# The up stage of a decoder step: the fourth Winograd product one block later and accumulated in PSUM, weight-quarter sums on VectorE instead of GpSimd

## The reference, cut to what matters

```python
def conv_ffn(hn, buf, w_up, conv_w, conv_b, w_down):
    T = hn.shape[1]
    up = hn @ w_up                                        # (T, 1024) @ (1024, 2 * 2816)
    full = jnp.concatenate([buf.astype(up.dtype), up], axis=1)
    conv = sum(full[:, j:j + T] * conv_w[j] for j in range(CONV_W)) + conv_b   # CONV_W = 3
    a, gt = jnp.split(conv, 2, axis=-1)
    return (a * jax.nn.silu(gt)) @ w_down, full[:, T:]
```

## Time and profile before

| | us |
|---|---|
| median of 3 runs | 2200.4 (2196.86 to 2200.54) |
| profiled execution, its own time | 2205.06 |
| its span, first to last instruction | 2203.1 |
| mean granted TensorE clock | 0.990 of full speed |
| VectorE busy | 1267.4 (58%) |
| ScalarE busy | 754.8 (34%) |
| GpSimd busy | 444.6 (20%) |

### The profile page before, as it was taken

The page is one execution under the profiler, slowest core; times in us unless marked ns, Lnnn a source line. Parts: engine busy times, 40 slices in busy tenths (PEclk is TensorE's granted clock), DMA queues, the critical chain, the costliest instruction groups (busy, mean ns, idle before and its releaser), DMA issues.

```text
span 2203.1 us, 35662 instructions
## 1 busy us (share of the span) xinstructions
PE 2145.4 (97%) x15110; PEld 2090.6 (95%) x15110; DVE 1267.4 (58%) x1576; ACT 754.8 (34%) x1094; POOL 444.6 (20%) x552
## 2 busy tenths in 40 slices
PE   7999999999999999999999999999999999999997
PEld 6999999999999999999999998999999999999997
DVE  6514756335456354236643233489999999864446
ACT  6313334333422322233322034254444444421113
POOL 6689920000000000000000000023232332200001
PEclk9999999999999999999999999999999999999999
DMA  7321215122431223245412143222222222343212
GB/s 274 120 76 65 69 45 186 50 88 78 146 109 67 87 79 108 87 144 180 142 43 77 58 173 154 96 74 72 81 67 81 67 80 82 130 154 125 86 67 77
DMA packets 66419, 222.78 MB, mean 101 GB/s; under 512 B 7584, under 2 KB 13136, under 8 KB 62576
## 3 DMA queue, kind: packets, MB, share of 16 engines
q1 hardware_dynamic: 46432, 130.15, 17.6%
q0 software_dynamic: 14688, 62.06, 7.5%
q10 hardware_dynamic: 5184, 28.98, 3.5%
HBM read 168.38 MB, written 51.78 MB: 100 GB/s over the span
## 4 chain that ended last, share of the span: by engine, by line
PE 71%; DVE 21%; issue 3%; ACT 2%; POOL 2%; DMA 1%; DVEq 0%; POOLq 0%; ACTq 0%
PE ps L305 19%; PE ps L308 19%; PE ps L306 19%; DVE WQ L3170 4%; DVE CA L3218 3%; DVE CA L3217 3%; POOL WX L2711 2%; PE ps L1981 1%; PE ps L2337 1%; PE ps L2313 1%; DVE UBG L2717 1%; DVE HOUT L3227 1%; DVE CA L3220 1%; DVE UBG L3210 1%; DMA WRAW<-in_wslabs 1%
## 5 line engine op out<-in xcount | busy, mean ns | idle before, releaser
L305 PE MATMUL ps<-XH,WH 128*128 128x352 f32 (+1 forms) x1752 | 567.1, 325 | 5.6 <-ACT STAGE L365 3.1
L306 PE MATMUL ps<-XL,WH 128*128 128x352 f32 (+1 forms) x1560 | 492.5, 321 | 0.0
L308 PE MATMUL ps<-XH,WL 128*128 128x352 f32 (+1 forms) x1752 | 371.5, 320 | 0.0
L305 PEld LDWEIGHTS ps<-XH,WH 128*128 128x128 f32 x1752 | 330.5, 189 | 14.3 <-issue 10.2
L299 DVE TENSOR_TENSOR WL<-WRAW,WH 128x1024 fp32r<-128x1024 f32 x133 | 166.7, 1253 | 271.7 <-ACT WH L294 270.2
L306 PEld LDWEIGHTS ps<-XL,WH 128*128 128x128 f32 x1560 | 294.8, 189 | 0.1
L308 PEld LDWEIGHTS ps<-XH,WL 128*128 128x128 f32 x1752 | 292.9, 189 | 0.0
L294 ACT ACTIVATE WH<-WRAW 128x1024 fp32r<-128x1024 f32 x133 | 140.8, 1058 | 330.0 <-PE ps L308 311.9
L305 PE MATMUL ps<-HX,WH 128*128 128x352 f32 (+1 forms) x480 | 153.6, 321 | 4.7 <-DVE HX L3231 3.7
L306 PE MATMUL ps<-HX,WH 128*128 128x352 f32 (+1 forms) x480 | 151.5, 321 | 0.0
L2777 PE MATMUL ps<-B,WQ 128*128 128x258 f32 x528 | 141.0, 288 | 2.9 <-DVE UBG L3210 2.4
(11 more groups left out here) (619 smaller groups left out, 4752.3 us busy)
## 6 DMA issues: line engine op xcount, KB each, us to landing
WRAW<-in_wslabs SPq DMA_DIRECT2D x133, 512.0 KB, 3.6
WRAW<-in_wup SPq DMA_DIRECT2D x88, 256.0 KB, 2.7
scratch_spill<-STAGE SPq DMA_DIRECT2D x40, 516.0 KB, 2.7
ZS<-scratch_spill POOLq DMA_DIRECT2D x24, 516.0 KB, 5.3
scratch_h<-HOUT ACTq DMA_DIRECT2D x22, 516.0 KB, 2.9
HRAW<-scratch_h POOLq DMA_DIRECT2D x22, 516.0 KB, 5.8
XIN<-in_xT SPq DMA_DIRECT2D x8, 516.0 KB, 4.6
XR<-in_xT ACTq DMA_DIRECT2D x2, 2064.0 KB, 8.6
```

The lines of the kernel that those rows point to most:

```text
L305: pe.matmul(out[t], WH[:, slot, w, :], xh(k, t), start=(k == 0), stop=False)
L306: pe.matmul(out[t], WH[:, slot, w, :], xl(k, t), start=False, stop=False)
L308: last = pe.matmul(out[t], WL[:, slot, w, :], xh(k, t), start=False, stop=(k == nk - 1))
```

## The change

- The four weight sums of each quad go from GpSimd to VectorE (`dve_sums`, `dve_late_sums`). A12 - WY is now made before A21 - A11. GpSimd keeps only DMA issues in the stage.
- P1, P6 and P7 of quad f add up in banks 4 and 5 for even f and in 6 and 7 for odd f. P4 of the same quad is added to the same banks, on top of P7. So ScalarE no longer takes P7 and VectorE no longer joins c.
- P4 of quad f runs one quad later, between P5 and P6 of quad f+1, after the join a3 of quad f has read the banks.
- The gate row is scaled in two parts: `scale_gate` its second half in SBUF after a3, `finish_gate` its first half straight out of PSUM after P4, late, between the two convolutions of VectorE's queue. `scale_first` is the value row's scale as before.
- TensorE's order is P1(f), P5(f), P4(f-1), P6(f), P3(f), P7(f), P2(f). It waits for finish_gate(f-2) before P1(f), for d2(f-1) before P5(f), for a3(f-1) before P4(f-1).
- The queues of ScalarE and VectorE are ordered anew, with the counts of the semaphores.

```diff
-            [("P1", 0), ("P5", 0), ("P6", 0), ("P2", 0), ("P3", 0), ("P7", 0), ("P4", 0), ("P1", 1), ("P5", 1),
...
+            [(p, f - (p == "P4")) for f in range(2, NF) for p in ("P1", "P5", "P4", "P6", "P3", "P7", "P2")] +
+            [("P4", NF - 1)])}
...
+        def bank_of(p, f):
+
+            return {"P5": 2, "P3": 2, "P2": 0}.get(p, 4 + 2 * (f % 2))
...
+        def dve_sums(dve, f):
+
+            dve.wait_ge(u_raw[1].sem, u_raw[1].at(16 * (f + 1)))
+            dve.wait_ge(u_raw[2].sem, u_raw[2].at(16 * (f + 1)))
             if f:
+                dve.wait_ge(s_lo, W_AT["P3", f - 1])
+            nc.vector.tensor_tensor(WX, A21, A22, ALU.add).then_inc(s_sum.sem, 1)
+            dve.wait_ge(u_raw[0].sem, u_raw[0].at(16 * (f + 1)))
             if f:
+                dve.wait_ge(s_lo, W_AT["P6", f - 1])
+            dve.wait_ge(s_sum.sem, s_sum.at(4 * f + 1))
+            nc.vector.tensor_tensor(WY, WX, A11, ALU.subtract).then_inc(s_sum.sem, 1)
+
+        def dve_late_sums(dve, f):
+
+            dve.wait_ge(u_raw[3].sem, u_raw[3].at(16 * (f + 1)))
+            dve.wait_ge(s_lo, W_AT["P5", f])
+            dve.wait_ge(s_sum.sem, s_sum.at(4 * f + 2))
+            nc.vector.tensor_tensor(WX, A12, WY, ALU.subtract).then_inc(s_sum.sem, 1)
+            nc.vector.tensor_tensor(A21, A21, A11, ALU.subtract).then_inc(s_sum.sem, 1)
...
+                for f in range(2, 4):
+                    pe.wait_ge(s_lo, i * 14 + W_AT["P1", f])
+                    pe.wait_ge(u_rb.sem, u_rb.at(i * 4 + (2 * f - 2)))
+                    product("P1", f)
+                    pe.wait_ge(s_lo, i * 14 + W_AT["P5", f])
+                    pe.wait_ge(u_dv, i * 6 + DV_AT["d2", f - 1])
+                    product("P5", f)
+                    pe.wait_ge(s_lo, i * 14 + W_AT["P4", f - 1])
+                    pe.wait_ge(u_dv, i * 6 + DV_AT["a3", f - 1])
+                    product("P4", f - 1)
+                    rest_of_quad(i, f)
...
             for f in range(1, NF):
-                act_product_hi(act, "P4", f)
+                more = f < NF - 1
+                if f > 1:
+                    act_product_hi(act, "P7", f)
+                    act_product_hi(act, "P2", f)
+                    act.wait_ge(u_cv.sem, u_cv.at(2 * f - 3))
+                else:
+                    act_take(act, "P1", 1, first_half(UB[1][0]))
+                    act_product_hi(act, "P6", 1)
+                    act_product_hi(act, "P3", 1)
                 now(f - 1, 0)
                 if f > 1:
+                    act_take(act, "P1", f, first_half(UB[f % 2][0]))
+                    if more:
+                        act_product_hi(act, "P1", f + 1)
                     act.wait_ge(u_cv.sem, u_cv.at(2 * f - 2))
...
+                act_take(act, "P5", f, second_half(UB[f % 2][1]))
+                if f == 1:
+                    act_product_hi(act, "P7", 1)
+                    act_product_hi(act, "P2", 1)
+                    act_product_hi(act, "P1", 2)
+                act_product_hi(act, "P4", f)
                 now(f - 1, 1)
...
+                act_take(act, "P6", f, second_half(UB[f % 2][0]))
+                if more:
                     act_product_hi(act, "P5", f + 1)
...
                 silu(f - 1)
...
+                if more:
+                    act_product_hi(act, "P6", f + 1)
                     act_product_hi(act, "P3", f + 1)
...
+            def scale_gate(f):
+                u = UB[f % 2][1][:, 2 + HALF:2 + N]
+                dve.wait_ge(u_dv, DV_AT["a3", f])
+                L(nc.vector.tensor_tensor(u, u, RB[:, HALF:N], M))
+
+            def finish_gate(f):
+                dve.wait_ge(u_pe, U_AT["P4", f])
+                nc.vector.tensor_tensor(first_half(UB[f % 2][1]), pair("P4", f), by_bank(RB[:, 0:HALF]), M).then_inc(u_rb.sem, 1)
...
             for f in range(1, NF):
+                more = f < NF - 1
+                dve_product_lo(dve, "P7", f)
+                dve_product_lo(dve, "P2", f)
+                if more:
+                    dve_product_lo(dve, "P1", f + 1)
+                convolve(f - 1, 0)
+                finish_gate(f - 1)
                 dve_product_lo(dve, "P4", f)
...
                 convolve(f - 1, 1)
...
+                if more:
+                    dve_sums(dve, f + 1)
                 else:
                     slab_lo(0)
...
+                join("d2", f)
+                if more:
+                    dve_product_lo(dve, "P5", f + 1)
+                    dve_late_sums(dve, f + 1)
+                product(f - 1)
+                if more:
+                    dve_product_lo(dve, "P6", f + 1)
+                else:
                     for kk in range(2):
                         rest_h(0, kk)
...
+                join("a3", f)
+                scale_gate(f)
+                if more:
+                    dve_product_lo(dve, "P3", f + 1)
                 else:
                     dve.wait_ge(u_pe, U_AT["P7", f])
                     slab_lo(1)
...
+                join("b", f)
+                scale_first(f)
             for kk in range(2, 4):
                 rest_h(0, kk)
             convolve(NF - 1, 0)
+            finish_gate(NF - 1)
             convolve(NF - 1, 1)
```

More of the change, by code:

```diff
@@ L2729, in pool_ffn @@
                 pool.dma_start(I["spill_x"][:, m, :], XR[:, m, :]).then_inc(xr_out.sem, 16)
[L2730 to L2734, removed]
-            pool.dma_start(O["buf1"], I["buf1"]).then_inc(gl_out, 16)
[L2736 to L2747, removed]
+            pool.dma_start(O["buf1"], I["buf1"]).then_inc(gl_out, 16)
+            pool.wait_ge(h_out.sem, h_out.at(16 * 4))
+            pool.wait_ge(u_pe, U_AT["P6", NF - 1])
+            for kk in range(2):
+                pool_load_h(pool, 0, kk)
+            pool.wait_ge(u_pe, U_AT["P3", NF - 1])
+            for kk in range(2, 4):
+                pool_load_h(pool, 0, kk)
             pool.wait_ge(h_out.sem, h_out.at(16 * 8))
@@ L2773, in product @@
                         k_wait(k)
-                    start, stop = k == 0 and p in ("P1", "P5", "P2", "P4"), k == 3
+                    start, stop = k == 0 and p in ("P1", "P5", "P2"), k == 3
                     for t in range(2):
-                        out, c = ps[:, PAIR[p] + t, 0:HALF // 2], slice(t * (HALF // 2), (t + 1) * (HALF // 2))
+                        out, c = ps[:, bank + t, 0:HALF // 2], slice(t * (HALF // 2), (t + 1) * (HALF // 2))
                         pe.matmul(out, w[:, 0, k, :], x[:, 0, k, c], start=start, stop=False, skip_group_check=True)
@@ L2802, in pe_ffn @@
             evacuated(pe, G_CO + 7)
-            product("P1", slot_of("P1", 0))
+            product("P1", 0)
             pe.wait_ge(s_lo, W_AT["P5", 0])
@@ L2820, in pe_ffn @@
             pe.wait_ge(u_ac, 3)
-            product("P7", slot_of("P7", 0), lambda k: pe.wait_ge(e_lo, E_AT["N3", k]))
+            product("P7", 0, lambda k: pe.wait_ge(e_lo, E_AT["N3", k]))
             norm_samples()
+            pe.wait_ge(s_lo, W_AT["P1", 1])
+            product("P1", 1)
             pe.wait_ge(s_lo, W_AT["P4", 0])
[L2824 to L2843, removed]
@@ L2844, in quad @@
                 if f == 1:
                     pe.wait_ge(norm_rb, 2)
[L2846 to L2853, removed]
-            pe.wait_ge(u_ac, 4 * NF)
+                product("P2", f)
+            rest_of_quad(0, 1)
+            with pe.Fori(0, (NF - 2) // 2) as i:
+                for f in range(2, 4):
[9 more added lines that the diff above has]
+                    rest_of_quad(i, f)
@@ L2856, in pe_ffn @@
+            pe.wait_ge(s_lo, W_AT["P4", NF - 1])
+            pe.wait_ge(u_dv, DV_AT["a3", NF - 1])
+            product("P4", NF - 1)
+            pe.wait_ge(u_rb.sem, u_rb.at(2 * NF - 2))
             pe.wait_ge(u_dv, DV_AT["b", NF - 1])
```

146 lines of the change are left out of this document (56 added, 90 removed).

## The result

| | before | after |
|---|---|---|
| median of 20 runs, us | 2200.26 (2196.86 to 2201.95) | 2203.23 (2199.07 to 2208.29) |
| ratio, 95% interval | | 1.0016 (1.0009 to 1.0023) |
| profiled execution's span, us | 2203.1 | 2199.6 |

The account below looks back on a forecast made before the run. VectorE's queue was taken to set the period, TensorE only following. Terms 1.7 + 2.1 + 1.6 - 0.1 - 1.6 = 3.7 us came off 2200.4, giving 2196.7 us; 8 in 10 range 2184 to 2209.

Parts of the forecast that it names:

- two round trips over ScalarE: Steady quad: VectorE waits for ScalarE's copy of P1(f+2), then for its gate convolution start; idle 1.20 and 0.79 us.
- GpSimd relief: Steady quad: VectorE instructions lengthened beside GpSimd's sums lose 3.0 us a quad, which goes once GpSimd computes nothing.
- three predicted waits: Steady quad: VectorE idle 1.20 us before rest P1 and 0.79 before the second convolution; TensorE's gap 0.7 before P7.
- the ring: Steady quad: the loop of VectorE's queue and its waits over ScalarE that sets the period, forecast at 21.00 us.
- number 3 of the new waits: Steady quad: VectorE's walk from second convolution to next scale_first at 21.00; period 21.09 to 21.00, 1.7 us gained.
- My own sign of being wrong: Steady quads: prediction wrong if the period is off by over 0.2 us, VectorE waits for DMA, or P7 waits drop the clock.
- The start: Start of the up stage: first convolution at 1489.05 instead of 1491.14, 2.1 us sooner, bounds 0 to 4.
- The end: Quad 21's first convolution to the down stage's third group, 32.57 us before: +0.14 us from changed round trips and waits.
- The clock's 1.6 us: Down stage after TensorE's wait for the first residual add: slow clock costs 1.6 us, between 0 and 2.
- The second: Rival: 0.7 us gap before P7 drops TensorE's clock; 2206 us, up to 2215; chance 0.12.
- The third: Rival: sums come late as VectorE waits for the third weight quarter; 2217 us; chance 0.10.
- The first: Rival: TensorE becomes the bound of the steady quads, period 20.3, 2183 us; chance 0.14.

Follow-up runs that it names:

- experiments 6 to 8: The changed kernel with ScalarE's take and copy of P1 moved earlier, with VectorE's finish_gate moved earlier, and with both: 2187.63, 2188.61 and 2178.96 us.
- experiment 9: The changed kernel with two more already met waits before the second sum (WY) of every quad: 2207.03 us, ratio 1.0031.
- experiment 10: The changed kernel with VectorE's queue reordered in the last quad only, first two residual adds between the last convolutions: 2198.17 us, ratio 0.9992.
- take_first: The changed kernel with take of P1(f) and copy of P1(f+1) ahead of the value row's convolution start in ScalarE's queue: 2187.63 us, ratio 0.9932.
- finish_early: The changed kernel with finish_gate(f-1) ahead of the value row's convolution in VectorE's queue: 2188.61 us, ratio 0.9947.
- both edits: The changed kernel with the edits of take_first and finish_early together: 2178.96 us, ratio 0.9907.
- sums-alone kernel: The kernel before with its order, banks and joins, only the four sums moved to VectorE: 2204.78 us, ratio 1.0019.

## Why the prediction was wrong, step by step

- **The mechanism of the steady quads was right.** VectorE's queue and its two round trips over ScalarE set the period, TensorE has one gap before P7, and the GpSimd relief was handed back. The three predicted waits of 1.20, 0.79 and 0.7 us measured 1.17, 0.72 and 0.75; that the two idle times lay on the ring is shown by experiments 6 to 8.
- **The step that failed is number 3 of the new waits, "next scale_first 21.00".** It came at 21.29. From scale to scale, worked out against measured: first convolution 4.15, 4.22; second 9.40, 9.46; WX 12.65, 12.74; WY 13.37, 13.56; d2 13.97, 14.18; late WX 15.29, 15.55; product 16.49, 16.76; rest P6 17.64, 17.91; scale 21.00, 21.29. The sums lost most: 0.10 at WY and 0.05 at late WX. I gave them the 0.72 of an instruction that waits for the one before it and for nothing else, while each of them also stands behind two met waits; at 0.03 us each (experiment 9) those would be 0.06 of the 0.10 at WY and all of the 0.05. The 0.07 at the first convolution and the rest, hundredths at other hand-overs, have no experiment. Over 20 steps (the last is 1.61 shorter, as worked out, and has the 0.29 too) that is 5.8 us, and it turns a period gain of 1.7 us into a loss of about 4 (21.29 against 21.09). A forecast of 0.09 us a quad from 25 steps read to 0.01 had no margin: my 0.1 a quad for the steady part was too narrow. My own sign of being wrong, a period off by over 0.2 us, came.
- **The start** was worth 1.7 us, not 2.1: 34.04 us from P1(0) to the first convolution (1484.98), 35.71 before. With the early slow stretch of experiment 10 it would be worth 0.1. The walk also lacked a wait of TensorE of 3.16 us in the first quad behind the start, and the slow stretch behind it (clock 0.57 from 1489 to 1497), against my "clock 1.00 in the stage":

```profile
1490.82 0.55 PE L2766 MATMUL ps<-N,WQ 128*128 128x258 f32 x1 [3.16 <-ACT UBA L2967]
```

  It cost nothing that shows: VectorE's steps from quad to quad are 21.29 from the first one on.
- **The end** was right to 0.03 us: 32.73 from quad 20's first convolution (1909.21) to the third down group, 32.57 before, so +0.16 for +0.14.
- **The clock's 1.6 us** came in one trace of the changed kernel (1.4) and not in the other. I put into the sum as certain what happens in a part of the runs.
- Together, for the traces: -3.7 + 5.8 + 0.4 - 0.2 = +2.3 with the slow stretch at the end (1.4 for 1.6), +0.9 without; against the mean of the two stages before, 747.6, they show +2.4 and +1.1. The medians' +3.0 lies in the interval of both comparisons; 0.6 to 1.9 of it is beyond the traces. The early slow stretch is a candidate, as it came in four of the eight traces of kernels with the changed start (the one of experiment 10, take_first, finish_early and both edits); it isn't shown for the changed kernel itself.
- **Profiled execution and median.** I carried a difference over to the median, which was sound, though the trace of before was 4.7 us late. Nothing in the sum leaned on that.
- **The rivals.** None came. The second, a clock swing from 0.7 us gaps in every quad, is refuted: with gaps of 0.75 the clock stayed at 1.00 from 1513 to 1880 us. So the Trainium skill's case of short idle times between groups of matmuls that make the clock swing ("TensorE: Matmul & The Clock Gate", "A second HAM failure mode: psum-queue depth-cycling") is not this one. The third didn't occur: VectorE never waited for a weight quarter. The first, TensorE as the bound at a period of 20.3 and 2183 us, is what take_first (20.27, 2187.6 us) and both edits (20.28, 2179.0 us) made of the kernel.

## What to carry to other kernels

When work leaves a contended engine, follow each in-order queue that it used to be beside: the gain of about 20 us was there, and in the old order one copy waiting ahead of one take in ScalarE's queue ate it, in the new order two round trips over ScalarE. In such a queue put what others wait for (takes out of PSUM, copies for the next block) ahead of what itself waits for a late result, and use the time that a round trip over another engine takes for independent work. A gain per block smaller than the hand-over costs left out of the walk is no forecast of a sign.

## What the runs showed of the hardware that I had not expected

- A wait on a count long reached isn't always free on VectorE: about 0.03 us each where the instruction also needs the result of the one just before it (0.82 to 0.88 us for two more). Where it doesn't, three waits cost nothing that shows (a step of 0.60 in the sums-alone kernel).
- Behind almost the same wait of TensorE, 2.32 and 2.28 us, the clock was once 1.00 and once 0.79 of full speed over 8 us, at a price of 0 and 1.4 us. Behind steady gaps of 0.75 us it was always 1.00. And a slow stretch came in four traces some 12 us behind P1(0), where TensorE had not waited at all since P1(0), at a price of 1.6 us.
- GpSimd's two-input sums lengthen VectorE instructions that start beside them, whether long (2.32 us for 1.28) or a copy of 10 columns (1.16 us for 0.17), so that shorter instructions beside them save nothing. But the joins, which read one operand from PSUM, were never lengthened: in three traces all 59 that started beside a sum took 0.68 or 0.69 us (VectorE and GpSimd, timelines, the kernel before):

```profile
1713.28 0.69 DVE L3210 TENSOR_TENSOR UBA<-UBA,ps 128x516 f32<-128x516 f32 x1
```
```profile
1712.89 1.62 POOL L2711 TENSOR_TENSOR WX<-WRAW,WY 128x512 f32<-128x512 f32 x1 [2.55 <-DVE WQ L3170]
```
